# The feature norms of a two-block transformer kernel: sums, root and reciprocal moved to one value per token

## What is computed

```python
def rms_norm(x, g):
    xf = x.astype(jnp.float32)
    y = xf * lax.rsqrt(jnp.mean(xf * xf, -1, keepdims=True) + NORM_EPS)
    return (y * g.astype(jnp.float32)).astype(x.dtype)

def modulate(h, shift, scale):
    return h * (1.0 + scale) + shift
```

## Time and profile before

| | |
|---|---|
| median of 3 runs | 2246.71 us (2243.39 to 2250.3) |
| profiled execution, span from first to last instruction | 2246.0 us |
| time outside that span | none recorded; the profile gives the span alone |
| TensorE busy | 2163.1 us (96%) |
| TensorE weight loads busy | 1514.0 us (67%) |
| VectorE busy | 1082.7 us (48%) |
| ScalarE busy | 462.0 us (21%) |
| mean granted TensorE clock | 0.993 |
| mean DMA rate | 129 GB/s |

### The profile page before, as it was taken

The page is one execution under the profiler, slowest core; times in us unless marked ns, Lnnn a source line. Parts: engine busy times, 40 slices in busy tenths (PEclk is TensorE's granted clock), DMA queues, the critical chain, the costliest instruction groups (busy, mean ns, idle before and its releaser), DMA issues.

```text
span 2246.0 us, 33411 instructions
## 1 busy us (share of the span) xinstructions
PE 2163.1 (96%) x14268; PEld 1514.0 (67%) x14268; DVE 1082.7 (48%) x1944; ACT 462.0 (21%) x1004; POOL 139.0 (6%) x148
## 2 busy tenths in 40 slices
PE   6999999989999999999998999999999999999998
PEld 3447878554688885456466885686785488768646
DVE  2675555477645446652353114585324428642443
ACT  2433211352300000031253000223210022311001
POOL 0004333000000000011100000002000000200000
PEclk9999999999999999999999999999999999999999
DMA  8221444504322224445103444333344433234441
GB/s 325 75 75 40 153 153 155 177 20 187 150 75 94 93 76 150 170 144 136 57 8 131 158 154 169 141 113 113 131 150 169 155 145 119 107 131 150 169 170 74
DMA packets 41665, 289.86 MB, mean 129 GB/s; under 512 B 5040, under 2 KB 6448, under 8 KB 7216
## 3 DMA queue, kind: packets, MB, share of 16 engines
q1 hardware_dynamic: 39344, 279.99, 34.0%
q0 software_dynamic: 1312, 3.15, 1.1%
q10 hardware_dynamic: 864, 4.61, 0.5%
HBM read 286.15 MB, written 1.05 MB: 128 GB/s over the span
## 4 chain that ended last, share of the span: by engine, by line
PE 91%; DVE 5%; ACT 2%; issue 1%; DMA 1%; SPq 0%; ACTq 0%; DVEq 0%
PE banks L1009 22%; PE banks L414 15%; PE banks L1571 12%; PE banks L1470 7%; PE banks L2726 6%; PE banks L2068 6%; PE banks L1751 2%; PE banks L1775 2%; PE banks L649 1%; PE banks L789 1%; PE banks L1771 1%; PE banks L2720 1%; PE banks L452 1%; PE banks L502 1%; PE banks L804 1%
## 5 line engine op out<-in xcount | busy, mean ns | idle before, releaser
L414 PE MATMUL banks<-normed,weight_ring 128*128 128x256 f32 (+1 forms) x1280 | 294.8, 393 | 7.8 <-DVE normed L566 5.7
L414 PEld LDWEIGHTS banks<-normed,weight_ring 128*128 128x128 f32 x1280 | 245.2, 192 | 56.7 <-issue 15.3
L1009 PE MATMUL banks<-arena 128*128 128x512 f32 x392 | 186.2, 593 | 0.7 <-DVE arena L1627 0.5
L1470 PE MATMUL banks<-normed,weight_ring 128*128 128x256 f32 x704 | 153.9, 382 | 3.4 <-ACT normed L580 3.4
L1009 PE MATMUL banks<-weight_ring,arena 128*128 128x512 f32 x338 | 157.1, 593 | 0.0
L1470 PEld LDWEIGHTS banks<-normed,weight_ring 128*128 128x128 f32 x704 | 134.9, 192 | 22.4 <-ACT normed L580 3.8
L1009 PEld LDWEIGHTS banks<-arena 128*128 128x128 f32 x392 | 74.1, 190 | 93.6 <-issue 92.3
L2726 PE MATMUL banks<-normed,weight_ring 128*128 128x256 f32 x576 | 127.6, 381 | 5.8 <-DVE normed L566 2.9
L2068 PE MATMUL banks<-normed,weight_ring 128*128 128x512 f32 x288 | 126.1, 593 | 0.0
L2726 PEld LDWEIGHTS banks<-normed,weight_ring 128*128 128x128 f32 x576 | 108.6, 190 | 22.6 <-issue 5.0
L974 DVE TENSOR_TENSOR arena<-weight_ring 128x512 f32<-128x512 f32 x67 | 46.2, 690 | 144.2 <-PE banks L1009 144.2
(11 more groups left out here) (455 smaller groups left out, 3422.4 us busy)
## 6 DMA issues: line engine op xcount, KB each, us to landing
weight_ring<-in_weights SPq DMA_DIRECT2D x266, 1024.0 KB, 4.8
residual<-in_tokens ACTq DMA_DIRECT2D x1, 2048.0 KB, 12.7
mix<-in_rpb POOLq DMA_DIRECT2D x32, 64.0 KB, 3.7
constants<-in_const ACTq DMA_DIRECT2D x1, 1953.5 KB, 12.6
out<-residual SPq DMA_DIRECT2D x1, 1024.0 KB, 4.8
branch<-arena POOLq DMA_DIRECT2D x1, 512.0 KB, 4.8
normed<-in_ple POOLq DMA_DIRECT2D x1, 512.0 KB, 3.7
vector_params<-in_vectors ACTq DMA_DIRECT2D x1, 223.0 KB, 5.8
```

The lines of the kernel that those rows point to most:

```text
L414: mm = pe.matmul(K.psum[lo:hi, banks[m % nb], 0:T], K.block(first[m] + k)[:, lo:hi], rhs(k), start=(k == 0), stop=(k == n_k - 1))
L1009: return pe.matmul(self.bank[i], left, b, start=(p == 0), stop=(p == n - 1))
L1470: mm = pe.matmul(K.bank(i % 4, T), K.block(first[i] + k), u[:, k, 0:T], start=(k == 0), stop=(k == KT - 1))
```

## The change

`scale_stage` is replaced by `row_norm`. The squared tile becomes the stationary side, in two halves of 128 tokens, and the moving side is one column of the ones matrix. The sum of a token then stands in that token's partition: one column in bank 1 for the first 128 tokens and one in bank 4 for the others. ScalarE takes the root of 128 x 2 values and VectorE the reciprocal of 128 x 2 values. Two transposes on TensorE, each of one column broadcast to 128, spread the factors over all partitions into bank 4, and VectorE multiplies with that bank as its operand, in place of a tile in SBUF. TensorE waits for the reciprocals inside the stage's own function, so the two transposes stand ahead of `product(7, 8)` and of `early_values`. The `embed` stage uses banks 0, 2, 3 and 5, since bank 1 is now written by the norm that follows.

```diff
     def scalar(act):
         need(act, deps)
...
+        act.wait_ge(sg["summed"].sem, at["summed"] + n)
+        act.activation(root, total, ACT.Sqrt, bias=K.c("eps"), scale=1.0 / D).then_inc(sg["rooted"].sem, 1)
 
     def tensor(pe):
...
-            for t in range(len(tiles)):
-                pe.wait_ge(squared.sem, sq + i + 1)
-                pe.matmul(K.bank(4 + g % 2, T), lhs, square[:, i % n_square, 0:T], start=(t == 0), stop=(t == len(tiles) - 1)).then_inc(summed.sem, 1)
-                i += 1
+        for i in range(n):
+            pe.wait_ge(sg["squared"].sem, at["squared"] + i + 1)
+            for t in range(nt):
+                mm = pe.matmul(K.psum[:, 1 + 3 * t, 0:1], square[:, i % n_square, t * P:t * P + P], K.c("ones")[:, 0:1], start=(i == 0), stop=(i == n - 1))
+            mm.then_inc(sg["summed"].sem, 1)
+        pe.wait_ge(sg["row_inverses"].sem, at["row_inverses"] + 1)
+        for t in range(nt):
+            mm = pe.transpose(K.bank(4)[:, t * P:t * P + P], inverse[:, t:t + 1].to_broadcast([P, P]), K.c("ident"))
+        mm.then_inc(sg["spread_inverses"].sem, 1)
 
     def vector(dve):
-        step = K.in_turn(dve, "vector")
-        for g in range(len(groups)):
-            dve.wait_ge(rooted.sem, ro + g + 1)
-            r = K.inverse[:, g % 2, 0:T]
-            step(dve.reciprocal(r, K.root[:, g % 2, 0:T]))
-            apply(dve, g, r, lambda ins: ins.then_inc(applied.sem, 1))
+        dve.wait_ge(sg["rooted"].sem, at["rooted"] + 1)
+        dve.reciprocal(inverse, root).then_inc(sg["row_inverses"].sem, 1)
+        dve.wait_ge(sg["spread_inverses"].sem, at["spread_inverses"] + 1)
+        apply(dve, K.bank(4, S), lambda ins: ins.then_inc(sg["applied"].sem, 1))
...
-            r = matmul_stage(K, KT, 2, lambda k, layer=layer: pT[:, layer, k, :], S, embed, r + [(p_ready, pb + 16)], who=lambda m: "vector")
+            r = matmul_stage(K, KT, 2, lambda k, layer=layer: pT[:, layer, k, :], S, embed, r + [(p_ready, pb + 16)], who=lambda m: "vector", banks=(0, 2, 3, 5))
```

More of the change, by code:

```diff
@@ L461, in token_stage, with row_norm @@
     return [(out, e + n_t)]
[L464 to L470, removed]
+def row_norm(K, tiles, apply, deps, n_apply, src_ready):
+    n, nt = len(tiles), S // P
+    counts = {"squared": n, "summed": n, "rooted": 1, "row_inverses": 1, "spread_inverses": 1, "applied": n_apply}
+    sg = {c: K.counter(c) for c in counts}
+    at = {c: sg[c].reserve(x) for c, x in counts.items()}
+    square = K.square.rearrange("p i (j n) -> p (i j) n", n=S)
@@ L471, in scale_stage @@
     n_square = square.shape[1]
-    sq, su, ro = squared.reserve(n if sums is None else 0), summed.reserve(n), rooted.reserve(len(groups))
-    ap = applied.reserve(n_apply or len(groups))
+    total, root, inverse = K.psum[:, 1:5:3, 0], K.token_root[:, 0:nt], K.token_inverse[:, 0:nt]
     def scalar(act):
         need(act, deps)
[L477 to L484, removed]
-                i += 1
[L486 to L489, removed]
@@ L491, in tensor @@
-    def tensor(pe):
[L492 to L499, removed]
-            for t in range(len(tiles)):
-                pe.wait_ge(squared.sem, sq + i + 1)
-                pe.matmul(K.bank(4 + g % 2, T), lhs, square[:, i % n_square, 0:T], start=(t == 0), stop=(t == len(tiles) - 1)).then_inc(summed.sem, 1)
-                i += 1
@@ L505, in vector @@
-    def vector(dve):
-        step = K.in_turn(dve, "vector")
-        for g in range(len(groups)):
-            dve.wait_ge(rooted.sem, ro + g + 1)
-            r = K.inverse[:, g % 2, 0:T]
-            step(dve.reciprocal(r, K.root[:, g % 2, 0:T]))
-            apply(dve, g, r, lambda ins: ins.then_inc(applied.sem, 1))
+        for i, src in enumerate(tiles):
+            if src_ready:
+                need(act, src_ready(i))
+            if i >= n_square:
+                act.wait_ge(sg["summed"].sem, at["summed"] + i - n_square + 1)
+            act.activation(square[:, i % n_square], src, ACT.Square).then_inc(sg["squared"].sem, 1)
@@ L513, in scale_stage @@
+    def vector(dve):
+        dve.wait_ge(sg["rooted"].sem, at["rooted"] + 1)
+        dve.reciprocal(inverse, root).then_inc(sg["row_inverses"].sem, 1)
+        dve.wait_ge(sg["spread_inverses"].sem, at["spread_inverses"] + 1)
+        apply(dve, K.bank(4, S), lambda ins: ins.then_inc(sg["applied"].sem, 1))
     K.add(scalar=scalar, tensor=tensor, vector=vector)
-    return applied, ap, [(applied, ap + (n_apply or len(groups)))]
+    return sg["applied"], at["applied"], [(sg["applied"], at["applied"] + n_apply)]
@@ L560, in modulated_norm, with apply @@
     halves = range(lo // S, 2) if T == T2 or lo else range(2)
-    def apply(dve, g, r, emit):
+    def apply(dve, r, emit):
         for k in range(KT):
@@ L567, in apply @@
             emit(ins)
-    applied, ap, ready = scale_stage(K, [[h[:, k, lo:lo + T] for k in range(KT)]], T, K.c("ones"), 1.0 / D, apply, deps, n_apply=KT, src_ready=src_ready)
+    applied, ap, ready = row_norm(K, [h[:, k, lo:lo + T] for k in range(KT)], apply, deps, KT, src_ready)
     if beside:
```

## The result

The changed kernel is slower: 2257.91 us median against 2249.34 in the same series (19 runs each), a ratio of 1.0038 with an interval of 1.0027 to 1.0049, so +8.5 us (6.1 to 11.0). The median lies inside the range on record, 0.1 us under its upper end of 2258, and outside the likeliest case's own 2243 to 2256; the change is over the 0.3% (6.7 us) within which that case put it. Runs of both kernels spread over 10 us and more: 2241.6 to 2257.7 before, 2249.3 to 2263.8 after, leaving out one run of each at over twice the time. The other eighteen of the changed kernel stand in two groups, five at 2249.3 to 2251.9 us with a mean clock of 0.986 or 0.987 and thirteen at 2257.0 to 2263.8 with 0.980 to 0.983; the profiled one is of the second group. In what follows a ratio is always to the kernel before, with its 95% interval.

A forecast was written before the change was run, and what follows sets the result against it. TensorE was taken to bound the kernel (91% of the chain that ended last), with time won where it idles or runs below full clock. Chain -7.0 and clock +9.8 give +2.8 on 2246.7: 2249.5 us, range 2231 to 2258.

The forecast's parts named there:

- likeliest case: All seven norms meet a clock fall; 2249.5 us, own range 2243 to 2256, chance 0.60.
- The chain: Sums to first scaled tile: six norms gain 1.32 us each, the second loses 0.9; -7.0 us in all.
- What the clock cost before: Low clock behind the first, third, fifth and seventh norms: 2.8 + 1.7 + 1.6 + 1.6 = 7.7 us in one execution.
- Where the falls come differs by execution: Assumption on norms in the kernel before: gaps of 2.8 us were seen both with and without a clock fall.
- What the clock costs after: A fall at each of seven norms, 7 x 2.5 = 17.5 us, 7.7 paid already: +9.8 us.
- twelfth of the 3.6 us: Allowance for sums run at half pace after a fall inside them: 0.3 us for each norm.
- 96-column stretch: 39 matmuls from 37.9 to 46.5 at clock 0.50, taken to show that busy loads don't bring the clock back.
- price of a load: From 32 records of 16 columns in 3.64 us: one sums record every 0.109 us at full clock.
- A: Rival: the clock holds at all norms as loads count as work; 2232.0 us, chance 0.24.
- B: Rival: clock falls come as often and cost the same as before; 2239.7 us, chance 0.07.
- C: Rival: clock falls before or at the start of each norm's sums, all at half pace; 2271.9 us, 0.09 with milder forms.
- the sums' bounds: Limits on the loss from half-pace sums in a norm: 0 and the whole 3.5 us.

The follow-up runs named there:

- filled: Kernel before plus 12 matmuls of 128 columns into an unread bank, behind the sums of the third to seventh norm: 0.9986, -3.1 us.
- 128 columns: Changed kernel with 128 moving columns of ones in the sums in place of one, column 0 read: 0.997, -6.7 us against the kernel before.
- narrow product widened: Sparse mixer's 16-column product (32 records, twice) given 128 moving columns: 0.9944 with 128-column sums, 0.9994 on the kernel before, 1.003 on the changed kernel.
- both clock edits: Kernel before with unread matmuls behind the third to seventh norm's sums and 128 moving columns in the sparse mixer's 16-column product: 0.9979.
- the split one: Kernel with 128-column sums, half of the second norm's work beside moved between sums and the wait for reciprocals, half behind the transposes: 0.996.

## Why the prediction came out as it did

To set the terms of the sum beside the traces, I took for each norm the time from the start of its first square until 100 matmul records that are not the norm's own (its own are sums, spreading transposes, filler) have started and the next one starts. Each column is from one trace, but for the stars, in us:

| norm | before | filled | after | 128 columns |
|---|---|---|---|---|
| 1 | 31.02 | 28.30 | 27.35 | 27.07 |
| 2 | 23.64 | 23.64 | 27.56 | 24.75 |
| 3 | 30.98 | 29.29 | 30.41 | 28.09 |
| 4 | 25.44 | 25.43* | 28.40 | 24.24* |
| 5 | 30.38 | 28.75 | 30.10 | 27.55 |
| 6 | 26.83 | 26.83 | 29.82 | 25.63 |
| 7 | 30.35 | 28.75 | 31.71 | 27.55 |

(* from the kernels that have the narrow product widened too, since its 16-column stretch lies inside this distance. The first norm of the filled kernel had no filler; it had no fall in that execution, nor in the one with both clock edits.)

*The chain.* Forecast: six times -1.32 and once +0.9, -7.0 us. Between the columns without falls: -1.23, +1.11, -1.20, -1.19, -1.20, -1.20, -1.20: -6.1. Its steps hold: from the end of the sums to the first scaled tile 1.02 us as forecast, root 0.26 for 0.295, transposes 0.43 for 0.39, scaling 0.48 us a tile, one every 0.39. The sums were taken as no gain and no loss, and with one column they are: 3.73 us where the clock is up, against 3.72. The 128-column sums of this comparison take 3.84, 0.11 us longer at each norm, so the chain that was forecast comes to -6.1 - 0.8 = -6.9 us. The second norm lost 1.0 for 0.9.

*What the clock cost before.* Forecast 7.7 us in the profiled execution. Before less filled: 2.72 + 1.69 + 1.63 + 1.60 = 7.6. Right for that execution, though the 2.72 of the first norm is not the filler's doing. The filled kernel's ratio puts the net gain at the five later norms at 3.1 us (0.7 to 5.6), beside the 4.9 of the profile; an average for all seven is therefore less sure than the term in the sum looked. The profile of the kernel before with the narrow product widened has its falls at the same four norms, so "Where the falls come differs by execution" is borne out by the first norm alone, which had none in the two filled kernels.

*What the clock costs after.* This is the term that was mis-sized. The step was "Seven norms: 7 x 2.5 = 17.5 us". After less 128 columns: 0.28 + 2.81 + 2.32 + 4.16 + 2.55 + 4.19 + 4.16 = 20.5, and 21.2 with the 0.11 us at each norm by which the 128-column sums are longer. (The changed kernel with the narrow product widened is a second execution with one-column sums; against the 128-column kernel with the same edit it pays 19.4, and 20.1 with the 0.11.) The terms for the norms were further off than their sum: the first was priced at 2.8 us and paid 0.4, because its fall, 579.2 to 582.6, slowed the work beside the norm, which else ends in a wait for the scaled tiles. In the three norms with a fall ahead of the end of the sums and 10 us of low clock it is 4.2, and there the "twelfth of the 3.6 us" for sums at half pace is where I went low: the seventh norm's sums lost 5.71 - 3.73 = 2.0 us by themselves. The transposes at half the clock, 0.69 us for 0.43, had no term either.

*The mechanism and its evidence.* The mechanism was the one forecast: TensorE busy with loads and hardly a moving column does not hold its clock. But the row that decided for it does not show it. The 96-column stretch of the earlier trace rows ends where the clock rises, and the same 64 records run on at full clock until 49.5. The next stretch of the kernel before, all 96-column records too:

```profile
46.60:49.30 2.70, 2.70 (x27) 2.70 (x25) 0.00 (x0) 0.00 (x0) 0.00 (x0) 1.00 0.85 348
```

So "not enough to bring the clock back" was wrong: it came back at 46.4, after 8.4 us with nothing else on TensorE, where the 256-column records behind the seventh norm had it after 3.3. What that row shows is a late rise, with 96 columns; that few columns beside the loads lose the clock was a guess until the runs with 1, 16, 64 and 128 columns. The forecast was lucky in this.

*What had no term.* Within the seven distances the profiles differ by +6.7 us (205.35 against 198.64), and the spans by 10.1. The other 3.4 lie at the narrow product (the low stretch from 1859), in the mixer at 1944 and, with the other sign, ahead of the first norm, which the changed kernel reached 2.9 us earlier. That the median was still within the range on record is luck: the change was +8.5 us where the sum said +2.8, and the kernel before stood at 2249.34 in that series in place of 2246.7, so 0.1 us was left. The prediction used the narrow product as the price of a load, noted that it kept 1.00 for 3.6 us between dense work, and did not see that it is itself a stretch that can lose the clock: in the earlier trace rows there is no sign of it, and the clock fell in it or right behind it in the profiles of six kernels: those with 1, 16, 64 and 128 columns in the sums, the filled and the split one. Code, order and data there are as before, so the change can act on these places by its timing alone. Whether the changed kernel falls there more often than the kernel before is not settled; widening the product helped it by no amount that can be told (1.003 against 1.0038).

*The rivals.* A, 2232.0 if the clock held, is nearly the kernel with 128 columns in both products (2234.49), and was out for the changed one. It was the right price for the wrong case. (It speaks of three long gaps ahead of the low stretches; the earlier trace rows has four norms with one.) The rule that I set beside it, that idle gaps between bursts are what lowers the clock (the Trainium skill, "TensorE: Matmul & The Clock Gate", "Why this matters for your kernels"), would fit here only if such loads did not count as work: the gaps of the seventh norm after are 0.55 and 0.57 us long, and the clock fell in the sums. B, the clock as before, is out too. C, every sum at half pace, came true in part for three norms, and by 0.2 us for the second. That transposes do not count as busy, the other rule that the prediction takes from the Trainium skill ("TensorE: Matmul & The Clock Gate", "Part 4: PE-mode transpose"), was not tried: with 128-column sums the two of them stood between two short gaps and the clock stayed at 1.00.

*The chances.* I gave "slower" 0.17, from C and the upper edge of my own case. The range of the case, +-4 us, came from the dense stretches alone. It should have carried the sums' bounds too, which I had written down as 0 to 3.5 us for each norm.

## What to carry to other kernels

Before a matmul is turned round so that few columns move, look at what TensorE does on both sides of it: here a chain of float32 loads cost the same time within 0.11 us with one moving column as with 64 or 128, and with one it cost the clock of the dense product behind it. Where the loads set the pace, try a moving side as wide as they allow, of which one column of the result is read: here that turned +8.5 us into -6.7. And when a change shortens a wait, count the quiet stretch from the last dense matmul to the next one, not the gaps alone.

## What the runs showed that I had not expected

The pace of float32 matmuls with a new 128 x 128 stationary tile each is the same for 1, 16, 64 and 128 moving columns, 3.73 to 3.84 us for 32 records at full clock. The granted clock is not: falls at all seven norms in each of the three profiles with 1 or 16 columns, and in the five with 64 or 128 at one norm of 35, the third of the split kernel. Single profiles differ by 4 us and more where the first norm begins, though all these kernels run the same code up to there: against the kernel before, the 128-column kernel was 1.6 us late and the changed one 2.9 us early, and over all twelve profiles the place moves by 5.6 us. That is over half of the 8.5 us that this study had to measure, so the times above rest on several runs of each kernel, and the profiles tell only where the time goes.
